# A hybrid decoder layer on one core: row sums carried in two more accumulator columns, and a last normalisation with squares alone on ScalarE for eleven of 17 tiles

## The chip, the cores and the metric

One program runs on one core of a Trainium2 chip. The metric is the device time of one execution in microseconds (us); the shown time is the median of three executions. The core's engines are TensorE (PE in the profile, its weight loads PEld), VectorE (DVE), ScalarE (ACT), GpSimd (POOL) and SyncE (SP), which here only issues DMA transfers.

## The reference, cut to what matters

The layer takes 2048 prompt rows and 8 sample rows of 1024 values. A mixer (spatial gating beside a state-space scan) is followed by an output projection and a layer normalisation that gives `x1`; then come a router and a mixture of 16 experts, and a last normalisation:

```
x   = layer_norm(ALPHA * x + mix, ln1_g, ln1_b)                      # x1
out = 0
for e in range(16):
    out += comb[:, e] * ((silu(x @ w_gate[e]) * (x @ w_up[e])) @ w_down[e])
y   = layer_norm(ALPHA * x + out, ln2_g, ln2_b)
# layer_norm: (z - mean(z)) * rsqrt(mean((z - mean)^2) + eps) * g + b, mean over 1024 columns
```

## The kernel before, in words

The program runs in stages. The ones that the change touches are the last two.

**Output stage** (about 460 to 690 us, `out_sync`, `out_gpsimd`, `out_scalar`). For each of 17 tiles of 128 rows (the first holds the 8 sample rows) VectorE normalises, ScalarE multiplies `x1` by ALPHA (`tile`, L1885) and SyncE stores the product in a DRAM tensor, `acc_dram` (`acc_rows` in the profile), whose rows are 1024 columns.

**Expert stage** (about 700 to 1183 us). The rows that each expert needs are listed in 48 tiles of 128 rows, padding included. Per tile GpSimd gathers the rows, TensorE transposes them, multiplies with gate and up weights (L2827) and the down weights (L2851). The product of 128 x 1024 lies in two PSUM banks; ScalarE copies the left half (L2698) and VectorE the right half (L2550) into `yo`, and GpSimd issues an indirect DMA that adds `yo` to the rows of `acc_dram` (L2413). Meanwhile ScalarE and VectorE split the next weights into high and low parts (L2653, L2510), VectorE makes the low part of the turned rows (`xg_low`, L2531) and of the turned hidden values (`ht_low`, L2544), for both of which TensorE waits.

**Last normalisation** (from 1183 us to the end). SyncE loads the finished rows back: the sample tile and four tiles into early space, and, once the weights' space is free, g and b and the other twelve (`rows_in`, L2357; one semaphore `acc_in[c]` for each tile). `ORDER` is the sample tile and then tiles 0 to 15; n counts places in this order, 0 to 16. The letter at place n in `KINDS` says who does what:

- N: VectorE takes mean and variance (`stats`, two BN_STATS on L2612, BN_AGGR, one small operation), subtracts the mean and multiplies by g (`centre`, L2625); ScalarE multiplies by 1/deviation (`scale`, L2742); GpSimd adds b (`shift`, L2436).
- P: as N up to `centre`; then TensorE multiplies by a diagonal matrix of 1/deviation and adds b (L2888, L2892) into PSUM; ScalarE copies the result back (`lift`, L2748).
- Q: as P, but ScalarE takes the statistics (`act_stats`: a pass for the sum, L2730, a small operation for minus the mean, L2732, and a pass for the squares, L2734). VectorE only turns them into the variance (L2608) and centres (L2623).
- S (in the changed kernel only): statistics as Q, the rest as N.

The work goes in pairs of places (0,1), (2,3) ... and 16 alone. On VectorE a pair is its statistics, then its two `centre`. On GpSimd it is one power (L2450, called the root here) for both 1/deviations, the diagonal matrix for a P or Q tile (`spread`, L2442, tile `diag`), then the `shift` of the pair before. ScalarE takes two Q tiles ahead, and then for a pair its scale, the lift of the pair before and one more Q tile. SyncE issues the 17 stores strictly in order, each when its tile is shifted or lifted. Each engine works its list in order, so one wait holds all that is behind it.

## Time and profile before

| | |
|---|---|
| median of 3 executions | 1230.56 us (1227.11 to 1231.9) |
| the profiled execution, its own time | 1230.92 us |
| its span, first to last instruction | 1229.3 us |
| PE busy | 1171.6 us, 95% |
| DVE busy | 880.7 us, 72% |
| ACT busy | 528.9 us, 43% |
| POOL busy | 479.1 us, 39% |
| mean granted TensorE clock | 0.983 |

Shares are over the whole span; the stages have different limits, and only the last 47 us see the work that the change is about.

### The profile page before, as it was taken

How to read it: one execution, taken by the hardware profiler on the slowest of the kernel's cores; microseconds unless marked ns; L12 is line 12 of the kernel's file. 1: busy time of each engine (PE TensorE's matmuls, PEld its weight loads, DVE VectorE, ACT ScalarE, POOL GpSimd, SP SyncE). 2: the span in 40 equal slices, each digit the busy share in tenths (PEclk: the TensorE clock that was granted, in tenths of full speed). 3: DMA queues.
4: the chain of work that ended last, by engine and by line, in shares of the span. 5: the costliest groups of instructions: out<-in, count | busy, mean ns of one | idle time of the engine just before them, and what ended most of it. 6: DMA issues, size and time to landing. Idle time of an engine off the chain costs nothing.

```text
span 1229.3 us, 23629 instructions
## 1 busy us (share of the span) xinstructions
PE 1171.6 (95%) x7094; PEld 981.8 (80%) x7095; DVE 880.7 (72%) x1911; ACT 528.9 (43%) x870; POOL 479.1 (39%) x591
## 2 busy tenths in 40 slices
PE   7999999999989989999998889999999999999976
PEld 6999999978878847888876878788878878888842
DVE  4466678568879857467877767777777777777766
ACT  4132111111103563223242356666666666666666
POOL 3106773100131206324233024554455554445446
PEclk9999999999989999999999999999999999999988
DMA  8689885685448674366798669898988889746496
GB/s 241 220 296 266 291 246 162 174 244 216 174 124 282 206 264 153 137 229 253 254 310 306 268 224 286 263 305 267 314 262 286 248 244 316 190 103 172 90 322 256
DMA packets 138840, 290.87 MB, mean 237 GB/s; under 512 B 49650, under 2 KB 67138, under 8 KB 127508
## 3 DMA queue, kind: packets, MB, share of 16 engines
q1 hardware_dynamic: 120404, 226.10, 52.7%
q0 software_dynamic: 17328, 61.80, 21.1%
q10 hardware_dynamic: 1040, 2.10, 0.5%
q8 instruction: 39, 0.64, 0.2%
q14 instruction: 29, 0.24, 0.1%
HBM read 178.49 MB, written 111.46 MB: 236 GB/s over the span
## 4 chain that ended last, share of the span: by engine, by line
PE 50%; DVE 5%; ACT 3%; issue 2%; POOL 1%; DMA 0%; ACTq 0%; DVEq 0%; POOLq 0%
PE p_out L2827 22%; PE p_out L2851 11%; PE p_out L2105 10%; PE p_x1t L2812 3%; PE p_x1t L2115 1%; PE p_parts L2836 1%; PE p_out L2892 1%; PE p_parts L2125 1%; ACT junk L2730 1%; POOL mixt_low L1801 1%; POOL rs L1806 0%; DVE x L2042 0%; DVE ya_r L2060 0%; DVE rowhot L2498 0%; ACT zi L2742 0%
## 5 line engine op out<-in xcount | busy, mean ns | idle before, releaser
L2510 DVE TENSOR_TENSOR wgu<-w_raw,wgu (+1 forms) x192 | 230.1, 1221 | 99.6 <-ACT wgu L2653 69.2
L2827 PE MATMUL p_out<-wgu,xg_high 128*128 x768 | 245.2, 400 | 5.3 <-issue 3.9
L2653 ACT CAST wgu<-w_raw x188 | 192.8, 1052 | 57.5 <-issue 56.6
L2827 PEld LDWEIGHTS p_out<-wgu,xg_high 128*128 128x128 f32 x768 | 139.3, 189 | 42.1 <-issue 16.4
L2827 PE MATMUL p_out<-wgu,xg_low 128*128 x384 | 150.6, 392 | 0.0
L2412 POOL TENSOR_TENSOR spare_e<-nothing 128x1 f32<-128x1 f32 x48 | 44.5, 927 | 214.5 <-DVE yo L2550 214.5
L2413 POOL DMA_INDIRECT acc_rows<-yo,si x48 | 111.9, 2331 | 9.1 <-issue 9.1
L2105 PE MATMUL p_out<-w_out_high,mixt_high 128*128 128x512 f32 x240 | 95.4, 397 | 0.0
L2105 PE MATMUL p_out<-w_out_low,mixt_high 128*128 128x512 f32 x240 | 93.9, 391 | 0.0
L2105 PE MATMUL p_out<-w_out_high,mixt_low 128*128 128x512 f32 x240 | 93.8, 391 | 0.0
L2827 PEld LDWEIGHTS p_out<-wgu,xg_low 128*128 128x128 f32 x384 | 72.1, 188 | 15.3
L2851 PE MATMUL p_out<-wd_high,ht_high 128*128 x192 | 80.8, 421 | 3.5 <-DVE ht_low L2544 3.5
L712 PE MATMUL pxs<-xt_high,w_xs_high 128*128 128x256 f32 (+1 forms) x256 | 75.3, 294 | 2.8 <-DVE xt_low L489 2.0
L2851 PE MATMUL p_out<-wd_high,ht_low 128*128 x192 | 76.5, 398 | 0.0
L2851 PE MATMUL p_out<-wd_low,ht_high 128*128 x192 | 76.3, 398 | 0.0
L1801 POOL TENSOR_TENSOR mixt_low<-ya,mixt_high 128x512 fp32r<-128x512 f32 x16 | 23.0, 1436 | 131.7 <-ACT mixt_high L1879 131.6
L2531 DVE TENSOR_TENSOR xg_low<-p_x1t,xg_high 128x512 fp32r<-128x512 f32 x96 | 61.7, 684 | 15.8 <-ACT xg_high L2640 15.4
L712 PE MATMUL pxs<-xt_high,w_xs_low 128*128 128x256 f32 (+1 forms) x256 | 73.0, 285 | 0.0
L712 PE MATMUL pxs<-xt_low,w_xs_high 128*128 128x256 f32 (+1 forms) x256 | 72.9, 285 | 0.0
L712 PE MATMUL pu<-xt_high,w_u_high 128*128 128x256 f32 (+1 forms) x256 | 72.4, 283 | 0.0
L712 PE MATMUL pu<-xt_high,w_u_low 128*128 128x256 f32 (+1 forms) x256 | 72.2, 282 | 0.0
L712 PE MATMUL pu<-xt_low,w_u_high 128*128 128x256 f32 (+1 forms) x256 | 72.2, 282 | 0.0
(507 smaller groups left out, 2834.0 us busy)
## 6 DMA issues: line engine op xcount, KB each, us to landing
w_raw<-in_w_gate SPq DMA_DIRECT2D x16, 1024.0 KB, 7.3
w_raw<-in_w_up SPq DMA_DIRECT2D x16, 1024.0 KB, 9.6
wd_high<-w_down_high SPq DMA_DIRECT2D x16, 1024.0 KB, 6.9
wd_low<-w_down_low SPq DMA_DIRECT2D x16, 1024.0 KB, 8.8
ya_u<-in_w_down SPq DMA_DIRECT2D x38, 256.0 KB, 4.8
w_down_low<-ya_r SPq DMA_DIRECT2D x38, 256.0 KB, 6.2
acc_rows<-ax SPq DMA_DIRECT2D x18, 512.0 KB, 6.7
xin<-in_x_prompt SPq DMA_DIRECT2D x16, 512.0 KB, 6.2
```

The costliest lines, as they stand in the source:

```text
L712: mm = t.matmul(banks[f % 2][:, 0:cols], (w_hi, w_lo)[h][w][:, k, f * P:(f + 1) * P], xt[x][i % 2][:, k, 0:cols], start=(k == 0 and x + h ...
L1801: gp.tensor_tensor(mixt[1][:, b, part, 0:n], src, mixt[0][:, b, part, 0:n].bitcast(F32), ALU.subtract).then_inc(mix_low, 1)
L2105: mm = t.matmul(po[b][m][0:n, :], mixt[x][:, b, k, 0:n], wo[w][:, k, m * SUP:(m + 1) * SUP], start=(k == 0 and x + w == 0), stop=(k == KD ...
L2115: mm = t.transpose(ptr[k // 4][:, k % 4, 0:n], x1[0:n, b, k * P:(k + 1) * P], ident[0:n, 0:n])
L2412: gp.tensor_tensor(spare[:], nothing[:], nothing[:], ALU.add)
L2413: gp.indirect_dma_start(acc_dram, bass.IndirectOffsetOnAxis(ap=si[:, b:b + 1], axis=0), yo[:, b, :], None, compute_op=ALU.add).then_inc(ad ...
L2510: low = tt(wgu[:, slot, 1, at], raw[:, slot, at], wgu[:, slot, 0, at].bitcast(F32), ALU.subtract)
L2531: low = tt(xl[:, b, part, :], pt_x[h], xh[:, b, part, :].bitcast(F32), ALU.subtract)
L2653: nc.scalar.copy(wgu[:, slot, 0, at], raw[:, slot, at]).then_inc(hi_set, 1)
L2812: mm = t.transpose(pt_x[k // 4][:, k % 4, :], xg[:, b, k:D:KD], ident[:])
L2827: mm = t.matmul(pg[b][:, :, :], x[:, b, k, :], w[h][:, k], start=(k == 0 and x is xh and h == 0), stop=(k == KD - 1 and x is xl))
L2851: mm = t.matmul(pd[m][:, :], ht[x][:, b, k, :], w[h][:, k, m * SUP:(m + 1) * SUP], start=(k == 0 and x + h == 0), stop=(k == 1 and x == 1))
```

## The change

`acc_dram` gets rows of 1026 columns. The two more columns start at zero (a new GpSimd memset and two small stores of zeros from SyncE). ScalarE's and VectorE's copies into `yo` also write the sum of their half into column 1024 and column 1025, so that the adding DMA carries them along. ScalarE's ALPHA product also writes its row sums, into `sum1`, which stays in SBUF. In the last normalisation VectorE makes minus the mean for a whole group of tiles from these sums (`means`, three small operations on 4, 5 or 7 columns); ScalarE's pass for the sum and its small operation are gone. `KINDS` becomes NPNQNQSQNQSQNQSQQ: places 6, 10 and 14 change from N to S and place 16 from P to Q, so VectorE takes BN_STATS for 6 tiles and not for 10, and ScalarE takes squares for 11 tiles and not for 7. Four of these are put ahead and not two; `junk` has two halves. The rows are loaded with 1026 columns, and some buffers move to make room.

```diff
-        acc_dram = dram("acc_rows", [SEQ + NS + 2 * P, D])
+        AW = D + 2
+        acc_dram = dram("acc_rows", [SEQ + NS + 2 * P, AW])
...
+                sp.wait_ge(zeros_set, 1)
+                sp.dma_start(acc_dram[0:SEQ + 2 * P, D:].rearrange("(t p) e -> p t e", p=P), zeros[:]).then_inc(sums_zero, 16)
+                sp.dma_start(acc_dram[SEQ + 2 * P:, D:], zeros[0:NS, 0, :]).then_inc(sums_zero, 16)
...
+                gp.memset(zeros[:], 0.0).then_inc(zeros_set, 1)
...
-                    nc.scalar.mul(ax1[0:n, b, :], x1[0:n, b, :], ALPHA).then_inc(ax1_set, 1)
+                    row = CH if c == 0 else c - 1
+                    nc.scalar.activation(ax1[0:n, b, :], x1[0:n, b, :], ACT.Copy, scale=ALPHA,
+                                         accum_out=sum1[0:n, row:row + 1]).then_inc(ax1_set, 1)
...
-            KINDS = "NPNQNQNQNQNQNQNQP"
+            KINDS = "NPNQNQSQNQSQNQSQQ"
+            FIRST_STATS = 4
+            GROUPS = ((0, EARLY), (EARLY, 9), (9, CH))
...
-                        sp.dma_start(row_of(c), acc_dram[c * P:c * P + n, :]).then_inc(acc_in[c], 16)
+                        sp.dma_start(summed_row(c), acc_dram[c * P:c * P + n, :]).then_inc(acc_in[c], 16)
...
-                    v.tensor_copy(yo[:, b, SUP:D], pd[1][:, :]).then_inc(yo_dve, 1)
+                    ts(yo[:, b, SUP:D], pd[1][:, :], 1.0, 0.0, ALU.mult, ALU.add, accum_out=yo[:, b, D + 1:AW]).then_inc(yo_dve, 1)
...
+                def means(lo, hi):
+                    for c in range(lo, hi):
+                        dve.wait_ge(acc_in[c], 16)
+                    rows = zi_early[:, lo:hi] if hi <= EARLY else zi[:, lo - EARLY:hi - EARLY]
+                    low = low2[:, lo + 1:hi + 1]
+                    fin(tt(low, rows[:, :, D], rows[:, :, D + 1], ALU.add))
+                    fin(tt(low, low, sum1[:, lo:hi], ALU.add))
+                    ts(low, low, -1.0 / D, None, ALU.mult).then_inc(mean_set, 1)
...
+                means(0, EARLY)
                 for n, cs in PAIRED:
                     for m in range(n, n + len(cs)):
                         stats(m)
                     if n == 0:
+                        means(*GROUPS[1])
                         dve.wait_ge(g_set, 2)
+                    if n == 2:
+                        means(*GROUPS[2])
                     for m in range(n, n + len(cs)):
                         centre(m)
...
-                    nc.scalar.copy(yo[:, b, 0:SUP], pd[0][:, :]).then_inc(yo_act, 1)
+                    nc.scalar.activation(yo[:, b, 0:SUP], pd[0][:, :], ACT.Copy, accum_out=yo[:, b, D:D + 1]).then_inc(yo_act, 1)
...
+                    if m > 2:
+                        act.wait_ge(ssq_set, m - 2)
                     act.wait_ge(acc_in[c], 16)
-                    nc.scalar.activation(junk[0:r, :], row, ACT.Copy, accum_out=sum2[0:r, n:n + 1]).then_inc(mean_set, 1)
-                    act.wait_ge(mean_set, 2 * m - 1)
-                    nc.scalar.mul(low2[0:r, n:n + 1], sum2[0:r, n:n + 1], -1.0 / D).then_inc(mean_set, 1)
-                    act.wait_ge(mean_set, 2 * m)
-                    nc.scalar.activation(junk[0:r, :], row, ACT.Square, bias=low2[0:r, n:n + 1],
+                    act.wait_ge(mean_set, 1 + [lo <= c < hi for lo, hi in GROUPS].index(True))
+                    nc.scalar.activation(junk[0:r, m % 2, :], row, ACT.Square, bias=low2[0:r, n:n + 1],
...
-                for n in AHEAD[:2]:
+                for n in AHEAD[:FIRST_STATS]:
                     act_stats(n)
```

On VectorE at places 2 and 3, before the change: the statistics of place 2 (`st`, `ag`, `var`), the variance of place 3 from ScalarE's squares (`ssq`), and the two `centre`.

```order
L2612 BN_STATS st_6285<-zi_early 128x6 x2
L2614 MEMSET spare_6292 128x1
L2615 BN_AGGR ag_6286<-st_6285 128x2
L2616 TENSOR_SCALAR var_6287<-ag_6286 128x1
L2608 TENSOR_SCALAR var_6287<-ssq_6291 128x1
L2625 SCALAR_TENSOR_TENSOR zi_early<-zi_early,ag_6286,p_x1t 128x1024
L2623 SCALAR_TENSOR_TENSOR zi_early<-zi_early,low_6290,p_x1t 128x1024
```

The same place after the change.

```order
L2638 BN_STATS st_6287<-zi_early 128x6 x2
L2640 MEMSET spare_6293 128x1
L2641 BN_AGGR ag_6288<-st_6287 128x2
L2642 TENSOR_SCALAR var_6289<-ag_6288 128x1
L2634 TENSOR_SCALAR var_6289<-ssq_6292 128x1
L2625 TENSOR_TENSOR low_6291<-zi 128x7
L2626 TENSOR_TENSOR low_6291<-low_6291,sum_6203 128x7
L2627 TENSOR_SCALAR low_6291<-low_6291 128x7
L2651 SCALAR_TENSOR_TENSOR zi_early<-zi_early,ag_6288,p_x1t 128x1024
L2649 SCALAR_TENSOR_TENSOR zi_early<-zi_early,low_6291,p_x1t 128x1024
```

Three small operations on the sums of seven tiles (tiles 9 to 15, the last group) now stand ahead of the two `centre` of places 2 and 3, and they wait for all seven tiles.

On ScalarE at the start of the last normalisation, before the change: two tiles with a pass for the sum, minus the mean and the squares, then the scale of place 0.

```order
L2698 COPY yo<-p_out 128x512
L2730 ACTIVATE junk,sum_6289<-zi_early 128x1024
L2732 ACTIVATE low_6290<-sum_6289 128x1
L2734 ACTIVATE junk,ssq_6291<-zi_early,low_6290 128x1024
L2730 ACTIVATE junk,sum_6289<-zi 128x1024
L2732 ACTIVATE low_6290<-sum_6289 128x1
L2734 ACTIVATE junk,ssq_6291<-zi,low_6290 128x1024
L2742 ACTIVATE zi<-zi,rstd_6288 8x1024
```

The same place after the change.

```order
L2728 ACTIVATE yo<-p_out 128x512
L2763 ACTIVATE junk,ssq_6292<-zi_early,low_6291 128x1024
L2763 ACTIVATE junk,ssq_6292<-zi,low_6291 128x1024 x3
L2770 ACTIVATE zi_sample<-zi_sample,rstd_6290 8x1024
L2763 ACTIVATE junk,ssq_6292<-zi,low_6291 128x1024
L2770 ACTIVATE zi_early<-zi_early,rstd_6290 128x1024
```

The passes for the sum and the small operations are gone, and four tiles' squares stand ahead of the first scale.

## Rows read from the trace of the kernel before

**Rows 1.** Windows: length, busy us (count) of PE PEld DVE ACT POOL, clock, DMA, GB/s

```profile
1197.50:1214.50 17.00, 12.13 (x29) 4.54 (x30) 16.61 (x36) 16.71 (x30) 14.17 (x13) 1.00 0.59 240
1214.50:1221.40 6.90, 6.90 (x10) 2.22 (x9) 5.33 (x10) 2.61 (x5) 5.95 (x6) 0.51 0.76 309
```

**Rows 2.** Timeline of VectorE, first statistics, pair (14,15), last centre: start, us, what

```profile
1182.91 1.26 DVE L2612 BATCH_NORM_STATS2 st<-zi 8x6 f32<-8x512 f32 x2
...
1212.93 1.28 DVE L2612 BATCH_NORM_STATS2 st<-zi 128x6 f32<-128x512 f32 x2
1214.25 0.20 DVE L2615 BATCH_NORM_AGGREGATE ag<-st 128x2 f32<-128x12 f32 x1
1214.49 0.15 DVE L2616 TENSOR_SCALAR var<-ag 128x1 f32<-128x1 f32 x1
1214.62 1.27 DVE L2625 SCALAR_TENSOR_TENSOR zi<-zi,ag,p_x1t 128x1024 f32<-128x1024 f32 x1
...
1218.63 1.27 DVE L2625 SCALAR_TENSOR_TENSOR zi<-zi,ag,p_x1t 128x1024 f32<-128x1024 f32 x1
```

**Rows 3.** Timeline of ScalarE: accumulator read, squares of one tile, last lift

```profile
1183.75 0.19 ACT L2730 ACTIVATION_READ_ACCUMULATOR junk<-zi_early 128x1 f32 x1
...
1184.21 1.15 ACT L2734 ACTIVATE junk<-zi_early,low 128x1024 f32<-128x1024 f32 x1
...
1223.89 1.07 ACT L2748 COPY zi<-p_out 128x512 f32<-128x512 f32 x2 [1.61 <-PE p_out L2892]
```

**Rows 4.** Timeline of GpSimd: root, diagonal and shift of a pair; last diagonal

```profile
1214.78 0.70 POOL L2450 TENSOR_TENSOR rstd<-var,half 128x2 f32<-128x2 f32 x1 [0.50 <-DVE var L2608]
1215.56 0.40 POOL L2442 TENSOR_TENSOR diag<-ident,rstd 128x128 f32<-128x128 f32 x1
1215.92 2.37 POOL L2436 TENSOR_TENSOR zi<-zi,b_row 128x1024 f32<-128x1024 f32 x1
1219.43 0.40 POOL L2442 TENSOR_TENSOR diag<-ident,rstd 128x128 f32<-128x128 f32 x1
```

**Rows 5.** Timeline of TensorE, the last two tiles

```profile
1217.38 3.78 PE L2892 MATMUL p_out<-zi,diag 128*128 128x512 f32 x4
1221.87 1.98 PE L2892 MATMUL p_out<-zi,diag 128*128 128x512 f32 x4
```

**Rows 6.** SyncE's issues, timeline: fifth and twelfth late row tile, last store

```profile
1169.81 0.66 SPq L2357 DMA_DIRECT2D zi<-acc_rows  x1
1176.56 1.75 SPq L2357 DMA_DIRECT2D zi<-acc_rows  x1
1224.99 0.33 SPq L2378 DMA_DIRECT2D out_y_prompt<-zi  x1
```

**Rows 7.** DMA view, narrow windows on these loads: us to landing last

```profile
zi<-acc_rows SPq DMA_DIRECT2D x1, 512.0 KB, 13.9
zi<-acc_rows SPq DMA_DIRECT2D x1, 512.0 KB, 21.0
```

**Rows 8.** DMA view: transfers issued at 482.69 and, third, 483.79; us to landing last

```profile
z<-in_x_prompt SPq DMA_DIRECT2D x1, 512.0 KB, 4.2
acc_rows<-ax SPq DMA_DIRECT2D x1, 512.0 KB, 5.7
```

**Rows 9.** DMA view, 1193:1197.6 and 1113.9:1115.6: packets, MB, share of 16 engines

```profile
q1 hardware_dynamic: 520, 1.85, 98.3%
...
q0 software_dynamic: 73, 0.24, 45.8%
```

**Rows 10.** Groups by line, x count, busy us, mean ns, idle before

```profile
L2550 DVE COPY yo<-p_out 128x512 f32<-128x512 f32 x48 | 32.9, 685 | 5.4 <-PE p_out L2851 5.4
L1885 ACT ACTIVATE ax<-x 128x1024 f32<-128x1024 f32 (+1 forms) x17 | 18.0, 1061 | 94.9 <-DVE x L2042 94.9
```

**Rows 11.** Timeline, one expert tile: VectorE's hand-off, TensorE's start

```profile
1166.97 1.29 DVE L2531 TENSOR_TENSOR xg_low<-p_x1t,xg_high 128x512 fp32r<-128x512 f32 x2 [0.26 <-ACT xg_high L2640]
1168.95 0.63 PE L2827 MATMUL p_out<-wgu,xg_high 128*128 x2
```

More of the change, by code:

```diff
@@ L1618, in hybrid_step @@
         scores = sb("scores", [P, TILES, E], where=late)
+        sum1 = sb("sum1", [P, TILES], where=late)
         GU = 2 * KD * FF
@@ L1651, in out_stage @@
             neg_half = sb("neg_half", [P, 1], where=pt)
+            zeros = sb("zeros", [P, CH + 2, 2], where=pt)
             assert pt.at <= base + 153 * KB, pt.at - base
@@ L1741, in stores @@
                     sp.wait_ge(ax1_set, p + 1)
-                    sp.dma_start(acc_dram[rows, :], ax1[:, b, :]).then_inc(ax1_stored[b], 16)
+                    sp.dma_start(acc_dram[rows, 0:D], ax1[:, b, :]).then_inc(ax1_stored[b], 16)
                 rows_in(0, 0)
@@ L2217, in hybrid_step @@
             xh, xl = sb("xg_high", [P, 2, KD, P], F32R, where=pt), sb("xg_low", [P, 2, KD, P], F32R, where=pt)
-            yo = sb("yo", [P, 2, D], where=pt)
+            yo = sb("yo", [P, 2, AW], where=pt)
             sl = sb("sl", [P, 2, FF], where=pt)
@@ L2228, in hybrid_step @@
             g2_row, b2_row = sb("g2_row", [P, D], where=rows), sb("b2_row", [P, D], where=rows)
-            rows = Place(nc, base + 32 * KB)
+            rows = Place(nc, base + 32 * KB + yo_over)
             st2, ag2 = sb("st2", [P, TILES, 2, 6], where=rows), sb("ag2", [P, TILES, 2], where=rows)
             var2, rstd2 = sb("var2", [P, TILES], where=rows), sb("rstd2", [P, TILES], where=rows)
-            sum2, low2, ssq2 = (sb(n, [P, TILES], where=rows) for n in ("sum2", "low2", "ssq2"))
+            low2, ssq2 = (sb(n, [P, TILES], where=rows) for n in ("low2", "ssq2"))
             spare2, half2 = sb("spare2", [P, 1], where=rows), sb("half2", [P, 2], where=rows)
@@ L2239, in hybrid_step @@
             wgu = sb("wgu", [P, 2, 2, GU], F32R, where=pt)
-            junk = sb("junk", [P, D], where=Place(nc, base + 43 * KB))
+            junk = sb("junk", [P, 2, D], where=Place(nc, base + 43 * KB))
             raw = sb("w_raw", [P, 2, GU], where=pt)
@@ L2243, in hybrid_step @@
             zi_at = base + 53 * KB + 2 * GU * 4
[L2244 removed]
             EARLY = 4
[L2246 to L2247 removed]
+            zi = sb("zi", [P, CH - EARLY, AW], where=Place(nc, zi_at + EARLY * D * 4 - 128))
+            zi_sample = sb("zi_sample", [NS, AW], where=Place(nc, base + 149 * KB))
+            assert early_at + EARLY * AW * 4 <= late_ones.at - P * 4 - 32
+            zi_early = sb("zi_early", [P, EARLY, AW], where=Place(nc, early_at))
             rows = Place(nc, zi_at)
@@ L2250, in hybrid_step, with summed_row @@
             diag = sb("diag", [P, 2, P], where=rows)
-            assert rows.at <= zi_at + EARLY * D * 4
-            b_both = sb("b_both", [2, D], where=Place(nc, zi_at + 3 * D * 4))
-            assert rows.at <= zi_at + 3 * D * 4
+            b_both = sb("b_both", [2, D], where=rows)
+            assert rows.at <= zi_at + EARLY * D * 4 - 128
+            assert zi_at + EARLY * D * 4 - 128 + (CH - EARLY) * AW * 4 <= base + 149 * KB
+            def summed_row(c):
+                return zi_sample[:, :] if c == CH else zi_early[:, c, :] if c < EARLY else zi[:, c - EARLY, :]
             def row_of(c):
-                return zi_early[0:tokens(c), c, :] if c < EARLY else zi[0:tokens(c), c, :]
+                return summed_row(c)[:, 0:D]
             pg = [po[1][i][:].rearrange("p (m f) -> p m f", m=2) for i in range(2)]
@@ L2758, in _ @@
                             lift(m)
-                    for m in AHEAD[n // 2 + 2:n // 2 + 3]:
+                    for m in AHEAD[n // 2 + FIRST_STATS:n // 2 + FIRST_STATS + 1]:
                         act_stats(m)
```

16 lines of the change are left out of this document (7 added, 9 removed).

## The prediction, made before the changed kernel was run

> **What bounds the kernel now.** I read the windows over the last 47 us first, then each engine's timeline there, then the DMA view of the row loads, and last the expert loop, where the change adds work.
>
> The windows [rows 1] show VectorE and ScalarE both full from 1197.5 to 1214.5 (16.6 and 16.7 of 17.0 us), GpSimd at 14.2 and TensorE at 12.1. VectorE works from 1182.9 to 1219.9 without a gap [rows 2]. A pair on it takes the 1.69 us from 1212.93 to 1214.62 for statistics, and two centres; the next pair starts 4.07 us later. Behind it GpSimd takes 3.54 us a pair: 0.78 from the root to the diagonal, 0.36 to the shift, and a shift of 2.4 [rows 4]. The last diagonal is ready at 1219.8 [rows 4], but TensorE is busy with place 15 until 1221.2, since its granted clock has fallen to the lower level (1.2 GHz): four products take 3.78 us there and 1.98 at the upper one (2.4 GHz) [rows 1, 5]. Products of place 16 from 1221.87 to 1223.85, its lift to 1224.96 [rows 3], its store issued at 1224.99 [rows 6]. A transfer of this size lands 4.2 us after its issue, and the third of a row issued almost together lands 2.6 us after the first, 1.3 each [rows 8]: 1224.99 and 4.2 is 1229.2, where the span ends.
>
> The DMA view holds what matters most. The fifth late tile (tile 8) lands 13.9 us after 1169.81, at 1183.7; the twelfth, tile 15, is issued at 1176.56 and lands 21.0 us later, at **1197.6** [rows 6, 7]. Now nobody minds: tile 15 is used at place 16, some 20 us later.
>
> **The change, part by part.**
>
> *VectorE's list.* Four tiles lose their own statistics. These take 1.63 us: from BN_STATS at 1212.93 to the small operation at 1214.49, and half of the 0.13 us to 1214.62, in which the pair's two small operations stand [rows 2]. The other half, 0.07, is what a variance from squares costs. That is 4 x (1.63 - 0.07) = 6.2 us less. Added are three group means. Each is three small operations, each waiting for the one before; a dependent pair of that kind starts 0.24 us apart (1214.25, 1214.49), so 0.65 us a group, 2.0 us in all. Left alone, VectorE ends 4.2 us earlier.
>
> *The wait it adds.* The order rows show the third group's means ahead of the centres of places 2 and 3, and they want tiles 9 to 15. VectorE comes there at 1182.9 + 0.65 + 2 x 1.65 (two N tiles) + 0.65 + 2 x 1.2 (centres) + 1.7 = 1191.6. Tile 15 lands at 1197.6. So VectorE stands for **6.0 us**, and behind it in its list stand every later centre and variance; ScalarE's scales, TensorE's products and GpSimd's roots wait for those. The loads can't come earlier by this change: they wait for the weights' space, which the loop frees. The second group (tiles 4 to 8) is complete at 1183.7, before VectorE asks at 1186.9, and costs nothing.
>
> *The path after it.* Means end at 1197.65 + 0.65 = 1198.3, centres of places 2 and 3 at 1200.7, statistics of 4 and 5 at 1202.4; GpSimd's root for them starts at 1202.5. From there VectorE needs three pairs of 4.07 and three pairs without BN_STATS of 2.5, 3.3 on average; GpSimd needs 3.54 for each. GpSimd sets the pace: its root for place 16 starts at 1202.5 + 6 x 3.54 = 1223.7, the diagonal is ready at 1224.8 (0.63 to it, 0.40 for it), five us later than now. VectorE has centred place 16 by 1222 (1202.4, two centres, 2.5 + 4.07 + 2.5 + 4.07 + 2.5, and the last 1.3). Products 1.98, to 1226.8; lift 1.07, to 1227.9. GpSimd's shift of place 14 ends at 1224.7 + 2.4 = 1227.1. So the stores of places 14, 15 and 16 are issued within a us, from 1227.2; the first lands 4.2 us on and the others 1.3 us apart: 1231.4, 1232.7, 1234.0. Against 1229.2 that is **+4.7 us** (bounds of this term: +3.5 if the last stores overlap better, +8.1 if the lower clock falls on the last products, which doubles their 2 us and the bias ahead of them).
>
> *ScalarE's list.* Seven passes for the sum with their small operation go, four squares of 1.15 and 0.19 us come [rows 3]. ScalarE has more room than before, and is not on the path. It hides under GpSimd; without that cover it would give back nothing either, since its squares wait for VectorE's means.
>
> *Rows of 1026 columns.* 0.2% more bytes, under 0.1 us. Rows no longer start at round addresses. Rows of 4096 bytes move at 98.3% of 16 engines for 1.85 MB in 4.6 us, 39 us of an engine for each MB; scattered rows of 1040 columns at 45.8% for 0.24 MB in 1.7 us, 52 us [rows 9]. The twelve loads (6.3 MB) would land between 0 and 5.2 us later by these two; they are whole and contiguous, as the first row is, so I take **+0.4**. The Trainium skill, DMA: Bandwidth & Descriptors, section How a descriptor splits into AXI transactions, says that a transaction starts at a 256-byte boundary and that bytes ahead of a descriptor's start are fetched and thrown away. By that rule, as an estimate, a row of 4104 bytes off the boundary costs up to 6% more, some 0.9 us on the loads instead of my 0.4; no row here separates it.
>
> *Copies into yo.* On ScalarE the accumulator read costs 0.19 us [rows 3]. VectorE's copy is 0.685 us [rows 10]; what an accumulating one costs no row shows. Below: nothing. Above: the same read, 0.19, on each of 48 tiles with TensorE waiting each time, 9.1 us. The hand-off shown has 0.69 us from the end of `xg_low` at 1168.26 to TensorE's start [rows 11], and TensorE doesn't wait; 0.2 us more fits. In tighter tiles some of it shows: I take **+0.3** for the loop.
>
> *Output stage.* 17 accumulator reads on ScalarE, 3.2 us, where ScalarE stands 94.9 us waiting ahead of these products [rows 10]; the memset and the 2312 zero pairs are small and early. **+0.1**, at most 3.2.
>
> Sum: 4.7 + 0.4 + 0.3 + 0.1 = +5.5 us. The profiled execution of before took 1230.92, of which 1.6 lie around its span; with the change 1236.4. The median of the runs shown is 0.36 lower, so **1236.0 us**, slower by 0.45%.
>
> **The rivals.**
>
> *A: the loads land in time.* If tile 15 were there at 1191.6, there would be no stall. Then VectorE ends at 1215.8, but GpSimd needs seven periods of 3.54 from 1191.7, and waits about a us in all at the pairs of 4.07: root of 16 at 1217.6, diagonal at 1218.6, shift of 14 at 1221; the last stores land at 1228.2 to 1228.7. The gain is 0.5 to 1 us: about **1230**. For it: only that the adding transfers that share the engines might run differently. Against it: the landing at 1197.6, and that these loads' trigger doesn't move. It decides only if the loads come more than 5 us earlier.
>
> *B: a low clock at the end, or late loads.* The clock fell at 1214.5 after a stretch in which TensorE was busy 12.1 of 17 us [rows 1]. The stall adds a gap of some 6 us after the products of place 1. If the lower level covers the last products, +3.4; if the loads are 2 us later, +1.6 beyond my term. About **1239**.
>
> *C: the loop pays.* VectorE's sum costs more than its room in the hand-offs, at 0.1 to 0.2 us a tile: 5 to 9 us over 48 tiles, and the stall on top: **1241 to 1245**. For it: no price of such an instruction in the trace. Against it: the 0.69 us of room.
>
> *D: the sums let some stage run faster by over 6 us.* Nothing in the rows gives that; the whole normalisation's saving on VectorE is 4.2.
>
> **How the numbers follow.** Forecast 0.52, A 0.12, B 0.20, C 0.12, D 0.04. A measurement of this kernel tells about 0.5%, 6.2 us, from no change. The forecast lies just inside that; a quarter of its chance lies beyond. So faster 0.04 (D), same 0.12 + 0.40 + a little of B = 0.55, slower 0.41. The range reaches down to A and up into C: 1229.5 to 1241.5; the forecast's own is 1233 to 1239.
>
> **What would show it.** In the changed kernel's trace: a gap of about 6 us on VectorE ahead of the means of seven columns, ended by the landing of tile 15; afterwards GpSimd without gaps at 3.5 us a pair, and VectorE with waits only on squares, if any; the last three stores issued within a us; TensorE's tiles in the loop at the same period as now. The forecast is wrong if tile 15 lands before 1193, if VectorE's copy into `yo` with its sum takes over 1.1 us, or if the last four products stand at the lower clock.

## The result, and the profile after

The changed kernel took **1262.41 us** (median of 4 executions, 1258.81 to 1266.63) beside 1231.23 for the kernel before: a ratio of 1.026 [1.023, 1.030]. It is slower by 31 us, on the side that had 0.41, but far outside the range of 1229.5 to 1241.5. The profiled execution took 1261.38 us, its span is 1259.8, 30.5 us over before; the rows below are of this execution. One execution of the kernel a_1040_loads below ran at a mean granted clock of 0.557 and took 1917.87 us; its row leaves it out.

First, windows of 10 us over the stage that the prediction passed in one line, the output stage, of the kernel after (columns as in [rows 1]; a share of over 1 counts packets that overlap):

```profile
490.00:500.00 10.00, 10.00 (x64) 8.30 (x65) 6.09 (x10) 3.00 (x7) 4.04 (x3) 1.00 1.87 61
500.00:510.00 10.00, 10.00 (x63) 8.08 (x63) 5.32 (x10) 1.96 (x5) 4.03 (x3) 1.00 0.80 13
510.00:520.00 10.00, 6.83 (x48) 5.23 (x46) 0.81 (x1) 0.00 (x0) 0.00 (x0) 1.00 1.00 66
520.00:530.00 10.00, 0.68 (x3) 0.68 (x4) 0.00 (x0) 1.82 (x5) 0.00 (x0) 0.51 0.92 220
530.00:540.00 10.00, 10.00 (x37) 8.02 (x38) 8.01 (x14) 3.88 (x8) 4.02 (x3) 0.81 0.78 229
```

The same windows of the kernel before:

```profile
490.00:500.00 10.00, 10.00 (x59) 8.04 (x57) 3.58 (x7) 1.19 (x2) 3.79 (x3) 1.00 0.43 121
500.00:510.00 10.00, 10.00 (x59) 8.32 (x50) 5.89 (x10) 3.03 (x6) 4.03 (x3) 1.00 0.47 182
510.00:520.00 10.00, 10.00 (x64) 8.08 (x62) 4.78 (x9) 3.53 (x8) 3.15 (x3) 1.00 0.41 160
520.00:530.00 10.00, 10.00 (x63) 8.12 (x62) 7.34 (x14) 3.55 (x7) 1.96 (x4) 1.00 0.62 221
```

The last two columns say it: from 500 to 510 the 16 engines are busy 0.80 of the time and move 13 GB/s, where before they move 182 with 0.47. I read full engines that move next to nothing as engines held up in their transfers; the trace doesn't show by what. TensorE, always full before, falls to 0.68 us of 10, and its clock to the lower level (0.51). What was issued just ahead stands in SyncE's timeline of the kernel after:

```profile
486.71 1.08 SPq L1754 DMA_DIRECT2D acc_rows<-zeros  x1
487.84 3.52 SPq L1755 DMA_DIRECT2D acc_rows<-zeros  x1
```

VectorE's timeline of the kernel after, the longest gap there (in brackets what ended it):

```profile
531.04 1.28 DVE L2031 SCALAR_TENSOR_TENSOR z<-z,p_out 128x512 f32<-128x512 f32 x2 [20.23 <-DMA z<-in_x_prompt]
```

And a piece of its chain of work that ended last (start, us, what):

```profile
492.84 35.04 DMA acc_rows<-ax
```

The two stores of zeros, 18.5 KB in 2312 pieces of 8 bytes, are issued at 486.7 and 487.8. A store of the ALPHA product behind them stands in the chain for 35.04 us (ScalarE waits 22.1 us for it, since it needs the buffer again), and the row load that VectorE waits for keeps it idle for 20.23 us. Before, VectorE waits for nothing longer than 4.6 us between 455 and 540, and that for a product of TensorE.

The second place is the end of the program. SyncE's timeline of the kernel after, the twelve late loads and the last store:

```profile
1185.63 16.90 SPq L2374 DMA_DIRECT2D zi<-acc_rows  x12
...
1254.77 0.33 SPq L2395 DMA_DIRECT2D out_y_prompt<-zi  x1
```

VectorE's timeline of the kernel after, the last `yo` copy and the means of the second and third group:

```profile
1202.98 0.69 DVE L2567 TENSOR_SCALAR_CACHE_REDUCE yo<-p_out 128x512 f32<-128x512 f32 x1 [3.98 <-DMA acc_rows<-yo,si]
1213.61 0.17 DVE L2625 TENSOR_TENSOR low<-zi 128x5 f32<-128x5 f32 x1 [6.23 <-DMA zi<-acc_rows]
1225.75 0.17 DVE L2625 TENSOR_TENSOR low<-zi 128x7 f32<-128x7 f32 x1 [7.52 <-DMA zi<-acc_rows]
```

GpSimd's timeline of the kernel after, the roots for places 4 and 5 and for place 16:

```profile
1230.48 0.69 POOL L2467 TENSOR_TENSOR rstd<-var,half 128x2 f32<-128x2 f32 x1 [8.68 <-DVE var L2634]
...
1249.80 0.56 POOL L2467 TENSOR_TENSOR rstd<-var,half 128x1 f32<-128x1 f32 x1
```

The gap that the prediction had put at 6.0 us is there, ahead of the means of seven columns, and it is 7.52. But it has company. The second group waits too, 6.23 us, where I had counted on none. VectorE's last `yo` copy waits 3.98 us for an add to land. The twelfth load lands just before 1225.75, which is 40 us after the first one's issue; before, it is 30 us from 1167.55 (the first late load's issue) to 1197.6 [rows 6, 7].

The two marks that divide the program are the start of the expert loop and the first late load. Timelines of VectorE and SyncE, before:

```profile
712.25 1.29 DVE L2531 TENSOR_TENSOR xg_low<-p_x1t,xg_high 128x512 fp32r<-128x512 f32 x2 [3.26 <-ACT xg_high L2640]
1167.55 10.76 SPq L2357 DMA_DIRECT2D zi<-acc_rows  x12
```

After, VectorE's (the late loads stand above, from 1185.63):

```profile
733.11 1.29 DVE L2548 TENSOR_TENSOR xg_low<-p_x1t,xg_high 128x512 fp32r<-128x512 f32 x2 [6.86 <-ACT xg_high L2670]
```

With the second half of the first pair as the mark, at 712.9 and 733.7, the 30.5 us divide in this way:

| stretch | before | after | difference |
|---|---|---|---|
| start to the first expert tile's `xg_low` | 712.9 | 733.7 | +20.8 |
| from there to the first late load's issue | 454.7 | 451.9 | -2.8 |
| from there to the end of the span | 61.7 | 74.2 | +12.5 |

The groups by line show what the sums cost on the copies into `yo` (after; columns as in [rows 10]):

```profile
L2567 DVE TENSOR_SCALAR_CACHE_REDUCE yo<-p_out 128x512 f32<-128x512 f32 x48 | 32.9, 685 | 6.9 <-DMA acc_rows<-yo,si 4.0 <-PE p_out L2879 2.9
L2567 DVE DVE_READ_ACCUMULATOR yo<-p_out 128x1 f32 x48 | 4.0, 83 | 0.0
L2728 ACT ACTIVATION_READ_ACCUMULATOR yo<-p_out 128x1 f32 x48 | 9.3, 193 | 0.0
```

VectorE's accumulating copy takes the same 685 ns as the plain one [rows 10], plus a read of 83 ns.

One gain is in the rows too. A `shift` on GpSimd takes 2.00 us in the kernel after, where it takes 2.37 before [rows 4]. The four kernels here whose row buffers in SBUF are 1026 columns wide (after, a_ride, a_ride_zeros, a_regroup) all have 2.00, and the other eleven, with 1024 or 1040 columns, have 2.36 to 2.37. The buffers also lie at other places, so the width is not shown to be the reason.

### The profile page after: what moved, and what is told of

It is laid out like the page before. It is cut to its first block, busy times and chain, and to the rows that moved or that the text cites. A ratio compares the mean times of both kernels' runs of the same rounds, so it can differ in the third digit from the quotient of the medians.

```text
span 1259.8 us, 23743 instructions
## 1 busy us (share of the span) xinstructions
PE 1172.1 (93%) x7094; PEld 984.1 (78%) x7095; DVE 878.4 (70%) x1952; ACT 529.2 (42%) x922; POOL 477.3 (38%) x592
## 3 DMA queue, kind: packets, MB, share of 16 engines
q10 hardware_dynamic: 1040, 2.10, 0.5%
## 4 chain that ended last, share of the span: by engine, by line
PE 45%; DMA 7%; DVE 4%; ACT 2%; SPq 2%; issue 2%; POOL 1%; ACTq 0%; DVEq 0%; POOLq 0%
PE p_out L2855 20%; PE p_out L2879 10%; PE p_out L2115 7%; PE p_x1t L2840 3%; DMA acc_rows<-ax 3%; DMA zi<-acc_rows 2%; DMA w_raw<-in_w_up 1%; SPq L2374 1%; PE p_out L2162 1%; PE p_parts L2864 1%; DMA x_rows<-comb 1%; PE p_out L2920 1%; POOL mixt_low L1808 1%; PE p_x1t L2125 1%; POOL rs L1813 1%
## 5 line engine op out<-in xcount | busy, mean ns | idle before, releaser
L2548 DVE TENSOR_TENSOR xg_low<-p_x1t,xg_high 128x512 fp32r<-128x512 f32 x96 | 61.8, 685 | 20.5 <-ACT xg_high L2670 19.3
L430 ACT ACTIVATE ya<-pu 128x256 f32<-128x256 f32 x32 | 12.2, 383 | 135.5 <-PE pu L713 135.5
```

What stands on the lines that cost most here:

```text
L2548: low = tt(xl[:, b, part, :], pt_x[h], xh[:, b, part, :].bitcast(F32), ALU.subtract)
```

## The experiments

All ratios are to the kernel before, run on the same chip beside it (medians 1230.3 to 1231.3). "Tail" is the time from the first late load's issue to the end of the span, "means of seven" the time from the same issue to where the work behind the third group begins; "first tile" is the start of the first `xg_low` pair's second half. These three are of one profiled execution each. In the kernels without the 2312 8-byte pieces and without stores of 4104-byte rows the first tile comes at 710.3 to 715.2, and in those that leave the last stage as it is the tail is 61.5 to 61.8: a difference of 3 us in the first column is near its scatter, one of 1 us in the last is not.

| kernel | median us | ratio, 95% interval | first tile | means of seven | tail |
|---|---|---|---|---|---|
| before | 1230.6 | 1 | 712.9 | (tile 15: 30.0) | 61.7 |
| after | 1262.41 | 1.0263 [1.0229, 1.0297] | 733.7 | 40.1 | 74.2 |
| b_zeros | 1236.02 | 1.0040 [1.0024, 1.0056] | 719.2 | | 61.5 |
| b_zeros64 | 1230.01 | 0.9997 [0.9983, 1.0010] | 712.0 | | 61.7 |
| b_off8 | 1230.57 | 1.0009 [0.9989, 1.0030] | 710.5 | | 61.5 |
| a_1040 | 1235.47 | 1.0042 [1.0027, 1.0057] | 712.8 | 30.8 | 66.5 |
| a_ride | 1243.76 | 1.0116 [1.0092, 1.0141] | 716.3 | 35.2 | 69.2 |
| b_wait | 1235.99 | 1.0054 [1.0032, 1.0075] | 710.3 | 29.7 | 68.5 |
| a_regroup | 1246.43 | 1.0133 [1.0111, 1.0155] | 725.7 | | 62.7 |
| a_1040_regroup | 1229.14 | 0.9993 [0.9980, 1.0006] | 712.9 | | 59.5 |
| b_loads8 | 1231.16 | 1.0004 [0.9988, 1.0020] | 711.5 | | 61.8 |
| a_ride_zeros | 1261.72 | 1.0258 [1.0221, 1.0295] | 732.5 | 40.2 | 74.3 |
| a_1040_loads | 1236.77 | 1.0046 [1.0029, 1.0062] | 715.2 | 30.8 | 66.5 |
| a_1040_adds | 1242.80 | 1.0088 [1.0058, 1.0118] | 713.8 | 38.7 | 74.5 |
| b_stores_1026 | 1236.80 | 1.0045 [1.0028, 1.0062] | 718.9 | | 61.6 |

### b_zeros: the kernel before with the zero stores alone

```diff
+        zero_dram = dram("zero_rows", [SEQ + NS + 2 * P, D + 2])
...
+                sp.dma_start(zero_dram[0:SEQ + 2 * P, D:].rearrange("(t p) e -> p t e", p=P), zeros[:]).then_inc(sums_zero, 16)
+                sp.dma_start(zero_dram[SEQ + 2 * P:, D:], zeros[0:NS, 0, :]).then_inc(sums_zero, 16)
```

> The kernel before, with only the zero stores added: the same two stores of 8 bytes a row, at a pitch of 4104 bytes, into a DRAM tensor of their own that nobody reads. If the first 18 us of the loss are the zero stores' work (theory Z), this is 12 to 20 us slower than before, with the step at the fourth tile of the output stage (VectorE waiting some 20 us for z). If they are due to the 1026-column rows (theory R), it is within 3 us of before.

Measured 1236.02 us, +0.4%. The windows of this kernel show the same hole, shorter than in the kernel after:

```profile
490.00:500.00 10.00, 10.00 (x59) 8.01 (x57) 3.58 (x7) 1.16 (x2) 3.76 (x3) 1.00 1.73 20
500.00:510.00 10.00, 10.00 (x57) 8.36 (x50) 5.86 (x10) 1.97 (x5) 4.03 (x3) 1.00 0.51 50
510.00:520.00 10.00, 4.54 (x38) 3.44 (x36) 0.00 (x0) 1.70 (x3) 0.00 (x0) 0.87 0.99 220
```

Two small stores to a tensor that nobody reads delay the program by some 5 us, with a wait of 14.06 us on VectorE for its row load. The kind of theory Z is right and its size is not: 5.7 us, between its 12 to 20 and the 3 of theory R. The DMA view from 484 to 490 us says when the pieces go out:

```profile
DMA packets 2526, 1.51 MB, mean 252 GB/s; under 512 B 2161, under 2 KB 2161, under 8 KB 2526
```

The packets under 512 bytes are the pieces: 2161 of the 2312 have their record in these 6 us, and the windows at 20 and 50 GB/s follow. So the traffic behind the pieces is slow as well, and for longer.

### b_zeros64: as many pieces, of 64 bytes

The same stores with rows of 1040 columns, so that each of the 2312 pieces is 64 bytes and starts at a multiple of 64.

```diff
-        zero_dram = dram("zero_rows", [SEQ + NS + 2 * P, D + 2])
+        zero_dram = dram("zero_rows", [SEQ + NS + 2 * P, D + 16])
```

> As b_zeros, but each of the 2312 pieces is 64 bytes and starts at a multiple of 64 bytes (pitch 4160). Theory P, that it is pieces smaller than and not filling what the memory writes at once: back within 3 us of before. Theory N, that it is the number of small pieces whatever their size: again 12 to 20 us slower.

Measured 1230.01 us, no change, and no hole in the windows:

```profile
490.00:500.00 10.00, 10.00 (x46) 8.19 (x44) 4.00 (x7) 1.83 (x3) 4.04 (x3) 1.00 0.52 168
500.00:510.00 10.00, 10.00 (x64) 8.18 (x63) 6.13 (x10) 3.02 (x6) 4.03 (x3) 1.00 0.50 184
```

Eight times the bytes in as many pieces cost nothing. So neither the number of pieces nor SyncE's time to issue them is the price. Two things differ between the kernels: the size of a piece, 8 or 64 bytes, and where it starts, every 4104 or every 4160 bytes. No run separates them, and none has a size in between, so that 64 bytes is the bound is not shown. The Trainium skill, DMA: Bandwidth & Descriptors, section Why small descriptors are slow (HBM only), names two costs of small pieces, a fixed overhead of some cycles for each packet and 32 bytes of metadata for each piece; both are the same for 8 and for 64 bytes, so by that section the pieces of 8 bytes should be no dearer. The measurement decides: b_zeros is 6 us slower.

### b_off8: the ALPHA product stored 8 bytes further on

Only these stores are shifted; adds and loads stay where they were, so the values are not the reference's. (The tensor's first 8 bytes get a small store of their own, for which SyncE waits.)

```diff
+        acc_flat = dram("acc_rows", [(SEQ + NS + 2 * P + 1) * D])
+        acc_dram = acc_flat[2:2 + (SEQ + NS + 2 * P) * D].rearrange("(r d) -> r d", d=D)
```

> The kernel before, where only the stores of the ALPHA products go 8 bytes beyond the rows' start (the adds and the loads go where they did, so the accumulated rows are shifted by two values and the output is not the reference's). Theory P: each row now has a broken piece at both ends, 256 a tile; at the rate of the zero stores in the changed kernel (2312 in about 33 us) that is up to 3.7 us of transfers behind each store; the output stage hides most of it, so 0 to 8 us slower, with the transfers issued behind each store landing 2 to 4 us later. If rows off by 8 bytes cost nothing: within 2 us and the same landings.

Measured 1230.57 us, no change. The median landing of these stores from 540 to 700 us goes from 7.9 to 8.9 us (DMA view of before, last column us to landing):

```profile
acc_rows<-ax SPq DMA_DIRECT2D x11, 512.0 KB, 7.9
```

The same row of this kernel:

```profile
acc_rows<-ax SPq DMA_DIRECT2D x11, 512.0 KB, 8.9
```

A shift that is the same for all rows costs nothing in time. The stores land 1.0 us later, less than the 2 to 4 us of theory P, although each of the 2312 rows now has a partial 64-byte piece at both ends.

### a_1040: the changed kernel with rows of 1040 columns

Everything of the change stays, but a row is 4160 bytes, a multiple of 64, and the zeros go out as 64 bytes a row. The late rows' buffer moves to make room, and GpSimd sets the idle columns of `yo` to zero once.

```diff
-        AW = D + 2
+        AW = D + 16
...
-            zeros = sb("zeros", [P, CH + 2, 2], where=pt)
+            zeros = sb("zeros", [P, 1, 16], where=pt)
```

> The changed kernel with rows of 1040 columns (4160 bytes, a multiple of 64) everywhere, the zeros stored as 64 bytes a row, and zeros in the 14 idle columns of yo. Theory P: both losses of the transfers go, and what is left is the wait for the third group's tiles: 1233 to 1240 us. If the wide rows as such, or the sums in yo, cost the rest: over 1245 us.

Measured 1235.47 us: the forecast of 1236.0, with the forecast's stall. In VectorE's timeline one gap is left, ahead of the third group:

```profile
1189.56 0.14 DVE L2635 TENSOR_SCALAR var<-ssq 128x1 f32<-128x1 f32 x1
1196.78 0.17 DVE L2626 TENSOR_TENSOR low<-zi 128x7 f32<-128x7 f32 x1 [7.08 <-DMA zi<-acc_rows]
```

In GpSimd's timeline the roots for places 4 and 5 and for place 16:

```profile
1201.51 0.69 POOL L2468 TENSOR_TENSOR rstd<-var,half 128x2 f32<-128x2 f32 x1 [8.25 <-DVE var L2635]
...
1222.26 0.56 POOL L2468 TENSOR_TENSOR rstd<-var,half 128x1 f32<-128x1 f32 x1
```

The width, 2 more columns or 16, is worth 27 us. The loads carry 1.6% more bytes than before, and the means of seven start 30.8 us after the first issue, where tile 15 had taken 30.0.

### a_ride: 1026 columns, no 8-byte stores

The zero columns ride in the ALPHA product, whose rows of 4104 bytes are stored whole.

```diff
-            ax1 = sb("ax1", [P, 2, D], where=pt)
+            ax1 = sb("ax1", [P, 2, AW], where=pt)
...
-                    sp.dma_start(acc_dram[rows, 0:D], ax1[:, b, :]).then_inc(ax1_stored[b], 16)
+                    sp.dma_start(acc_dram[rows, :], ax1[:, b, :]).then_inc(ax1_stored[b], 16)
```

> The changed kernel with its rows of 1026 columns, but no separate stores of zeros: the two zero columns ride in ScalarE's ALPHA product, whose rows of 4104 bytes are stored whole and without gaps. Theory (the 2312 pieces of 8 bytes hold up the output stage, and the late loads are slow because rows start off round addresses, so partial pieces are written and read there too): the output stage is back at the times of before within 3 us, the late loads are still late (the last one lands over 24 us after its issue), the whole 1240 to 1247 us. Rival 1 (all of it comes from the 8-byte pieces, the late loads too): 1235 us, like the kernel with rows of 1040 columns. Rival 2 (the gaps between rows are not the matter, rows of 4104 bytes off round addresses cost everywhere): the output stage still loses over 8 us, the whole over 1250 us.

Measured 1243.76 us, as the theory has it, 19 us below the changed kernel and 8 above a_1040. Rows of 4104 bytes cost on their own: 2.7 us in the tail, and in the output stage 3.5 us, which is near the scatter of that mark. In the DMA view of 540 to 700 us the stores land after 12.8 us:

```profile
acc_rows<-ax SPq DMA_DIRECT2D x11, 513.0 KB, 12.8
```

And in its timeline VectorE stands 2.62 and 8.25 us ahead of the second and third group; the first late load was issued at 1170.0:

```profile
1192.31 0.17 DVE L2621 TENSOR_TENSOR low<-zi 128x5 f32<-128x5 f32 x1 [2.62 <-DMA zi<-acc_rows]
1205.19 0.17 DVE L2621 TENSOR_TENSOR low<-zi 128x7 f32<-128x7 f32 x1 [8.25 <-DMA zi<-acc_rows]
```

### b_wait: the group wait alone

```diff
+                    if n == 2:
+                        for c in range(9, CH):
+                            dve.wait_ge(acc_in[c], 16)
```

> The kernel before with one thing alone: VectorE waits for the loads of tiles 9 to 15 ahead of the centres of places 2 and 3, where the change's third group of means stands. Theory (my term of the stall): VectorE stands some 7 us from 1190.2 to the landing of tile 15 at 1197.6, and, with ten tiles of its own statistics, is the bound behind it; the end moves by 5 to 7 us: 1236 us, ratio 1.004 to 1.006. Rival (the loads have spare time and the engines catch up): ratio within 0.002 of 1.

Measured 1235.99 us, ratio 1.0054. VectorE stands 7.06 us:

```profile
1195.31 1.28 DVE L2625 SCALAR_TENSOR_TENSOR zi_early<-zi_early,ag,p_x1t 128x1024 f32<-128x1024 f32 x1 [7.06 <-DMA zi<-acc_rows]
```

The wait on seven tiles at place 2 is worth what it was forecast to be. Here the tail grows by 6.8 us, about the whole stall, and nothing catches up behind it; in a_1040, where VectorE has less to do, it grows by 4.8, beside the 4.7 of the prediction.

### a_regroup and a_1040_regroup: the third group split

```diff
-            GROUPS = ((0, EARLY), (EARLY, 9), (9, CH))
+            GROUPS = ((0, EARLY), (EARLY, 9), (9, 12), (12, CH))
...
-                    if n == 2:
-                        means(*GROUPS[2])
+                    if n in (4, 8):
+                        means(*GROUPS[1 + n // 4])
```

> The changed kernel with its third group of means split in two, tiles 9 to 11 at place 4 and tiles 12 to 15 at place 8. Theory (three causes of the loss: 8-byte zero pieces 17 us, loads landing 10 us late, the group wait behind them): the gap on VectorE before the third group shrinks, since it then asks only for tiles that are nearly in; the output stage stays 17 us late. 1248 to 1254 us. Rival (the gap was only a shadow of loads that the last places wait for anyway): 1259 us or more.

> The changed kernel with rows of 1040 columns, whose zeros are stored as whole pieces of 64 bytes, and with the third group of means split as in the kernel beside it. Theory: nothing is left of the three losses; VectorE does not stand, GpSimd sets the pace at 3.5 us a pair from about 1190: 1228 to 1231 us, ratio 0.997 to 1.001, as rival A of the prediction. Rival (something else in the changed kernel costs as well, the squares on ScalarE or the loop): 1233 us or more.

a_regroup measured 1246.43 us, 16 below the changed kernel and below my 1248 to 1254. The tail is 11.5 us shorter (62.7 and not 74.2): the 7.5 us wait is gone, the second group waits 3.26 us and not 6.23 (VectorE's timeline):

```profile
1203.97 0.17 DVE L2625 TENSOR_TENSOR low<-zi 128x5 f32<-128x5 f32 x1 [3.26 <-DMA zi<-acc_rows]
```

The rest is in the output stage, which this edit doesn't touch: the first expert tile comes at 725.7 and not 733.7, of which the loop gives back 2.8. The delay behind the zero stores is thus not a fixed number; two programs with the same stores there had 13 and 21 us.

a_1040_regroup measured 1229.14 us, ratio 0.9993 [0.9980, 1.0006]: rival A's time, the fastest of all here, and not to be told from the kernel before. Its tail is 59.5 us, 2.2 shorter than before and clear of the 61.5 to 61.8 of the kernels that leave it alone. In the median 1 to 2 us can't be told from nothing, so a gain by the whole change is not shown. VectorE takes the three small operations in passing:

```profile
1194.56 0.14 DVE L2635 TENSOR_SCALAR var<-ssq 128x1 f32<-128x1 f32 x1
1194.62 0.15 DVE L2626 TENSOR_TENSOR low<-zi 128x3 f32<-128x3 f32 x1
1194.81 0.18 DVE L2627 TENSOR_TENSOR low<-low,sum 128x3 f32<-128x3 f32 x1
1195.03 0.17 DVE L2628 TENSOR_SCALAR low<-low 128x3 f32<-128x3 f32 x1
1195.10 1.27 DVE L2652 SCALAR_TENSOR_TENSOR zi_early<-zi_early,ag,p_x1t 128x1024 f32<-128x1024 f32 x1
```

### Which transfers of 4104-byte rows are slow

Four kernels take this apart: b_loads8 and a_1040_loads change only the late loads, a_1040_adds only the adds, b_stores_1026 only the stores of the ALPHA product.

```diff
-                        sp.dma_start(row_of(c), acc_dram[c * P:c * P + n, :]).then_inc(acc_in[c], 16)
+                        o = 2 * (EARLY <= c < CH)
+                        sp.dma_start(row_of(c), acc_flat[c * P * D + o:(c * P + n) * D + o].rearrange("(r d) -> r d", d=D)).then_inc(acc_in[c], 16)
```

That was b_loads8. In the next two `rows_1026` is the same DRAM tensor seen as rows of 1026 columns; a_1040_loads:

```diff
+                        if EARLY <= c < CH:
+                            sp.dma_start(summed_row(c)[:, 0:D + 2], rows_1026[c * P:c * P + n, :]).then_inc(acc_in[c], 16)
+                            continue
```

a_1040_adds:

```diff
-                    gp.indirect_dma_start(acc_dram, bass.IndirectOffsetOnAxis(ap=si[:, b:b + 1], axis=0),
-                                          yo[:, b, :], None, compute_op=ALU.add).then_inc(added[b], 16)
+                    gp.indirect_dma_start(rows_1026, bass.IndirectOffsetOnAxis(ap=si[:, b:b + 1], axis=0),
+                                          yo[:, b, 0:D + 2], None, compute_op=ALU.add).then_inc(added[b], 16)
```

b_stores_1026, where `ax1` is 1026 columns wide too:

```diff
-                    sp.dma_start(acc_dram[rows, :], ax1[:, b, :]).then_inc(ax1_stored[b], 16)
+                    sp.dma_start(rows_1026[rows, :], ax1[:, b, :]).then_inc(ax1_stored[b], 16)
```

> The kernel before with one thing alone: the twelve late loads read rows of 4096 bytes that start 8 bytes further on in the accumulator tensor, so their output is not the reference's; stores and adds are as before. Theory (rows off round addresses make the loads themselves slower): the last load lands 33 to 36 us after the first one's issue, and not 30.0; the time hardly moves, since tile 15 has 20 us of spare time: ratio within 0.003 of 1. Rival (the adding transfers of 4104-byte rows, which are still under way when the loads start, delay them): 30 us as before.

> The changed kernel with rows of 1040 columns, of which the twelve late loads alone read the accumulator tensor as rows of 4104 bytes (their values are then not the reference's). Theory L (reading rows of 4104 bytes is slow): the last load lands some 35 us after the first one's issue, the group wait on VectorE grows from 7.1 to 12 us, and the time from 1235.5 to about 1240 us. Rival (the loads are late since other transfers of 4104-byte rows slow them): 30 to 31 us and 1235 us.

> The same kernel of 1040 columns, whose adding transfers alone treat the tensor as rows of 4104 bytes (the output is not the reference's; tile 15 and the sample tile are loaded from rows whose adds are over). Theory A (adds of 4104-byte rows are slow and hold up the loads beside them): the last adds land after 12 us and not 9.1, the last load 34 to 35 us after the first one's issue, 1240 us. Rival: adds as before, last load at 30 to 31 us, 1235 us.

> The kernel before whose ALPHA product alone is stored as rows of 4104 bytes without gaps (the adds and loads keep rows of 4096 bytes, so the output is not the reference's). Theory (stores of rows that start at ever another 8 bytes are slow, where a fixed shift of 8 bytes took 7.6 us): these stores land after 12 us as in the kernel with riding columns, and not 6.7, the later output stage falls behind by about 3 us: ratio 1.002 to 1.003. Rival: 7.6 us or less, ratio within 0.001 of 1.

**Loads: no.** Shifted by 8 bytes, the last one lands 30.5 us after the first issue, and 1231.16 us is no change; my theory at that point, that the loads themselves were slow, fell. With rows of 4104 bytes (a_1040_loads, ratio 1.0046 beside the 1.0042 of a_1040) it is 30.8 us from the first issue at 1170.2 to the means, as in a_1040, and the gap in VectorE's timeline 6.95:

```profile
1200.96 0.17 DVE L2631 TENSOR_TENSOR low<-zi 128x7 f32<-128x7 f32 x1 [6.95 <-DMA zi<-acc_rows]
```

**Adds: yes.** In a_1040_adds the loads are the aligned ones, and yet the means of seven start 38.7 us after the first issue; the tail is as long as that of the changed kernel (74.5, 74.2), with the same three gaps in VectorE's timeline. The time is 1242.80 us, more than the 1240 of theory A; the profile has no landing for these adds, so its 12 us can't be compared:

```profile
1183.13 0.69 DVE L2571 TENSOR_SCALAR_CACHE_REDUCE yo<-p_out 128x512 f32<-128x512 f32 x1 [3.53 <-DMA acc_rows<-yo,si]
1191.66 0.17 DVE L2629 TENSOR_TENSOR low<-zi 128x5 f32<-128x5 f32 x1 [4.14 <-DMA zi<-acc_rows]
1205.14 0.17 DVE L2629 TENSOR_TENSOR low<-zi 128x7 f32<-128x7 f32 x1 [8.86 <-DMA zi<-acc_rows]
```

The size of this delay is no fixed number either: a_ride, with the same adds, has 35.2 us and a tail of 69.2.

**Stores: yes.** In b_stores_1026 they land after 12.7 us (7.9 before), the first expert tile comes 6.0 us late, the time is 1236.8, twice the loss that I had expected. Its DMA view of 540 to 700 us:

```profile
acc_rows<-ax SPq DMA_DIRECT2D x11, 513.0 KB, 12.7
w_down_high<-yb_r SPq DMA_DIRECT2D x23, 256.0 KB, 9.4
```

The second row shows that the weights' stores beside them, which nobody has touched, take 9.4 us and not 6.8. The row of before:

```profile
w_down_high<-yb_r SPq DMA_DIRECT2D x23, 256.0 KB, 6.8
```

### a_ride_zeros: the 8-byte stores back, in a tensor of their own

The kernel of a_ride and the two stores of b_zeros.

> The kernel whose zero columns ride in the ALPHA product, with the two stores of 2312 pieces of 8 bytes put back, but into a DRAM tensor of their own. Theory (the 8-byte pieces cost some 8 us wherever they go, as in the kernel before with them; what the changed kernel loses beyond that in its output stage comes from pieces and rows that share a 64-byte stretch): first expert tile 7 to 10 us later than with the riding columns alone, at 723 to 727: 1250 to 1254 us. Rival 1 (the delay of the pieces grows with what is queued behind them, whatever rows they lie in): first expert tile at 731 or later, 1259 us or more. Rival 2 (no addition, the losses overlap): first expert tile at 720, 1246 us.

Measured 1261.72 us, the time of the changed kernel. The numbers are those of rival 1: it doesn't matter which rows the zeros lie beside, so pieces of zeros and rows that share 64 bytes are not the cause. That the delay grows with what is queued behind the pieces, as rival 1 has it, no run tests. The same 2312 pieces cost 5 us among rows of 4096 bytes (b_zeros) and 18 us (1261.7 less 1243.8) among rows of 4104. The windows show the hole: three of them under 70 GB/s (23, 29 and 68), where b_zeros has two:

```profile
500.00:510.00 10.00, 10.00 (x64) 8.08 (x63) 6.12 (x10) 1.97 (x5) 4.03 (x3) 1.00 0.65 29
510.00:520.00 10.00, 4.92 (x39) 3.67 (x37) 0.00 (x0) 0.00 (x0) 0.00 (x0) 0.94 1.02 68
```

The clock falls only in the windows in which TensorE runs dry and in those behind them: 0.94 and 0.55 here, 0.87 and 0.79 in b_zeros, 0.51 and 0.81 in the kernel after. I take it as a result of the hole.

## Why the prediction was wrong

**The step that failed** stands under *Output stage*: "the memset and the 2312 zero pairs are small and early. **+0.1**, at most 3.2." The stores are small (18.5 KB) and early (at 487 us), and the first expert tile comes 16 us later with them (732.5 in a_ride_zeros, 716.3 in a_ride). By the ratios of these two the zero pieces cost 17.5 us (medians 18.0), where the prediction had 0.1. I had priced them by bytes and issue time, and looked for what waits for the zeros (only SyncE, at the end of the stage) and not for what is queued beside and behind them. The bound was wrong as well: it came from ScalarE's accumulator reads alone, and no row bounded a write of 8 bytes.

**The second step** is *Rows of 1026 columns*, "they are whole and contiguous, as the first row is, so I take **+0.4**", with 5.2 at most. I took it as a matter of the loads. There the step holds: reads at odd addresses cost nothing in time (b_loads8, a_1040_loads). The same rows are also added and stored, and those writes cost 5.7 us (a_1040_adds against a_1040, 0.0046 of 1231) and 5.5 us (b_stores_1026). Both together cost 9.1 (a_ride against a_1040, 0.0074 of 1231; 8.3 by the medians). The intervals of the ratios are 2 to 4 us to each side, so the two may simply add up or overlap in part. In rival A I even named "the adding transfers that share the engines" as something that might run differently, and gave it no price. The rule on the start of a transaction that I had set beside this term at 0.9 us (the Trainium skill, DMA: Bandwidth & Descriptors, section How a descriptor splits into AXI transactions) is one for reads. The runs neither bear it out nor refute it: rows of 4160 bytes don't all start at multiples of 256 either, so a_1040_loads and a_1040 can be alike, and both have the means of seven 30.8 us after the first issue, 0.8 us later than tile 15 landed before.

**The wait it adds: right.** 6.0 us forecast, 7.06 to 7.08 measured in b_wait and a_1040, 7.52 in the changed kernel. Counted from the first late load's issue, VectorE was to come at 24.1 us and tile 15 at 30.0; in a_1040 it is 23.7 and 30.8. That the second group "costs nothing" is right with timely loads, and 6.23 us in the changed kernel.

**The path after it: right in a_1040, only in part in the changed kernel.** From the end of the third means to GpSimd's root of places 4 and 5 I had 4.2 us; it is 1226.3 to 1230.5. GpSimd's period was to be 3.54 us. In a_1040 it is 3.46 (roots at 1201.51 and 1222.26), GpSimd is busy 20.32 of 20.80 us there, and the chain that ended last runs over its roots and shifts: the mechanism as forecast. In the changed kernel the period is 3.22, from 1230.48 to 1249.80, since a shift takes 2.00 us. There the chain runs over ScalarE, which has no gap from 1237.3 to 1251.9, although I had written that it "is not on the path". The lower clock came as well, on products in the middle and not on the last ones: four of them took 3.75 us at 1228.85 (granted clock 0.50 from 1226.3 to 1230.5) and 1.93 at 1251.72. In the working, VectorE has two pairs of 4.07 us left behind place 5 and not three; the sum for place 16 uses two, so nothing hangs on it. The sum of stall and path gave 1236.0, and a_1040, which is the change without the two costs of the writes, has 1235.47. That these agree to half a us is in part luck: the stall was 1.1 us longer than forecast, and six periods together half a us shorter.

**Copies into `yo`, the loop: right.** The stretch is 2.8 us shorter than before, not longer, and 451.9 to 456.0 us over all kernels here, so +0.3 can't be told from nothing; rival C's price of 0.1 to 0.2 us a tile is 0.083 on VectorE, and doesn't show in the loop.

**Rivals.** B's "late loads" came true in kind, at 10 us and not 2. A came true once the group was split and the rows aligned. The whole by runs, in ratios to the kernel before: 5.2 us for the wait (a_1040), 9.1 more for adds and stores of 4104-byte rows (a_ride), 17.5 more for the zero pieces (a_ride_zeros). That these add up to the loss follows from a_ride_zeros having the time of the changed kernel; it is no test of each. The delays vary from program to program (35.2 and 38.7 us to the means of seven, 13 and 21 us in the output stage), so the two larger terms hold for these kernels alone.

## What to carry to other kernels

When a change widens a row or adds a small store, read the sizes and starts of what is *written* to DRAM in bytes. Here 2312 pieces of 64 bytes cost nothing, and 18.5 KB in pieces of 8 bytes held the core's DMA traffic under 70 GB/s for 20 to 30 us, though no engine that computes waits for the pieces. Rows of 4160 bytes and not 4104, zeros included, took back 27 of 31 us. And a wait on a whole group of loads is priced at its latest member: ask for each only as late as its first use, which was worth another 6 us here, enough to bring the change back to the time of before.
